# Operand tiles with 32 unused bytes behind each row tile

## The reference

```
u = rmsnorm(h) @ w_in            # 2048 x 5632
ya = silu(layernorm(conv31(a_val * sigmoid(a_glu)))) * silu(a_z)
yb = window_attention(q, k, v) * silu(b_z)
h = h + concat(ya, yb) @ w_out   # 2048 x 2048
h = h + rmsnorm(p @ w_pe) * sigmoid(h @ w_pg)
```

## Time and profile before

| | |
|---|---|
| median of 3 runs | 1776.14 us (1776.02, 1776.14, 1781.95) |
| span of the profiled execution | 1780.4 us |
| TensorE busy, weight loads | 1759.6, 1678.8 us |
| VectorE, ScalarE, GpSimd busy | 1312.3, 899.0, 39.9 us |
| DMA | 326.07 MB, 183 GB/s |

### The profile page before, as it was taken

How to read it: one execution, slowest core, us unless ns; L and a number is a source line. 1 busy time by engine, 2 the same in 40 slices (tenths; PEclk the granted TensorE clock), 3 DMA queues, 4 the chain that set the end, 5 groups by cost and what they waited for, 6 DMA issues and landing times.

```text
span 1780.4 us, 35691 instructions
## 1 busy us (share of the span) xinstructions
PE 1759.6 (99%) x14349; PEld 1678.8 (94%) x14349; DVE 1312.3 (74%) x2087; ACT 899.0 (50%) x1326; POOL 39.9 (2%) x48
## 2 busy tenths in 40 slices
PE   8999999999999999999999999999999999999997
PEld 8999999999999999999999899898989999999876
DVE  7899899976779987998677765556565657566754
ACT  5433665545544355556465454545455443655653
POOL 0000000000000000000000110000100000000000
PEclk9999999999999999999999999999999999999999
DMA  7666545555656665456556656665655566455553
GB/s 232 187 206 193 190 143 174 192 188 185 192 177 209 192 199 151 146 186 206 189 191 197 201 179 203 187 189 170 206 162 170 190 190 193 142 158 169 172 189 130
DMA packets 200082, 326.07 MB, mean 183 GB/s; under 512 B 14911, under 2 KB 66319, under 8 KB 199821
## 3 DMA queue, kind: packets, MB, share of 16 engines
q1 hardware_dynamic: 197085, 320.85, 58.0%
q10 hardware_dynamic: 2864, 3.36, 0.6%
HBM read 320.42 MB, written 2.69 MB: 181 GB/s over the span
## 4 chain that ended last, share of the span: by engine, by line
PE 86%; DVE 9%; ACT 1%; issue 1%; DMA 1%; ACTq 0%; DVEq 0%; SPq 0%
PE g L495 67%; PE g L506 11%; DVE w_lo L902 4%; DVE cacc L1148 3%; PE att L620 2%; PE att L641 2%; PE att L596 2%; DMA turned<-q 1%; ACT w_hi L1531 1%; ACTq L1519 0%; PE att L793 0%; DVE u L996 0%; DMA stage<-in_w_in_dram 0%; ACT L1540 0%; DVE q L923 0%
## 5 line engine op out<-in xcount | busy, mean ns | idle before, releaser
L902 DVE TENSOR_TENSOR w_lo<-stage,w_hi 128x1024 fp32r<-128x1024 f32 x577 | 707.6, 1234 | 388.8 <-ACT w_hi L1531 388.1
L1531 ACT CAST w_hi<-stage 128x1024 fp32r<-128x1024 f32 x577 | 598.2, 1050 | 595.3 <-PE g L495 373.7
L495 PE MATMUL g<-a_hi,w_hi 128*128 128x256 f32 x2496 | 703.9, 282 | 2.4 <-DVE w_lo L902 1.5
L495 PE MATMUL g<-a_hi,w_lo 128*128 128x256 f32 x2496 | 695.0, 278 | 0.0
L495 PE MATMUL g<-a_lo,w_hi 128*128 128x256 f32 x2496 | 694.9, 278 | 0.0
L495 PEld LDWEIGHTS g<-a_hi,w_hi 128*128 128x128 f32 x2496 | 472.1, 189 | 11.8 <-issue 9.5
L495 PEld LDWEIGHTS g<-a_lo,w_hi 128*128 128x128 f32 x2496 | 470.6, 189 | 0.0
L495 PEld LDWEIGHTS g<-a_hi,w_lo 128*128 128x128 f32 x2496 | 469.7, 188 | 0.5 <-issue 0.2
L495 PE MATMUL g<-b_hi,w_hi 128*128 128x256 f32 x1440 | 403.6, 280 | 0.4 <-DVE w_lo L902 0.3
L495 PE MATMUL g<-b_hi,w_lo 128*128 128x256 f32 x1440 | 400.4, 278 | 0.0
L495 PE MATMUL g<-b_lo,w_hi 128*128 128x256 f32 x1440 | 400.4, 278 | 0.0
(11 more groups left out here) (230 smaller groups left out, 1368.1 us busy)
## 6 DMA issues: line engine op xcount, KB each, us to landing
stage<-in_fox_w_in_dram SPq DMA_DIRECT2D x128, 512.0 KB, 3.8
stage<-in_w_in_dram SPq DMA_DIRECT2D x112, 512.0 KB, 3.8
stage<-in_swa_w_in_dram SPq DMA_DIRECT2D x72, 512.0 KB, 3.9
stage<-in_w_in_dram SPq DMA_DIRECT2D x128, 256.0 KB, 3.1
stage<-in_w_out_dram SPq DMA_DIRECT2D x64, 512.0 KB, 4.2
stage<-in_w_pg_dram SPq DMA_DIRECT2D x64, 512.0 KB, 3.9
stage<-in_fox_w_out_dram SPq DMA_DIRECT2D x32, 512.0 KB, 4.5
stage<-in_swa_w_out_dram SPq DMA_DIRECT2D x32, 512.0 KB, 4.0
```

Source lines behind the costliest of these rows:

```text
L495: mm = pe.matmul(acc[:, j * S:(j + 1) * S], w[:, slot, c0 + j * P:c0 + (j + 1) * P], xx[:, k, :], start=st and m == 0 and j % 2 == 0, stop ...
L902: dve.tensor_tensor(w_lo[:, slot, :], stage[:, slot, :], w_hi[:, slot, :].bitcast(F32), ALU.subtract).then_inc(*t.inc("w_split"))
L1531: act.copy(w_hi[:, slot, :], stage[:, slot, :]).then_inc(*t.inc("w_rounded"))
```

## The change

```diff
+SKEW = 8
 ...
         sb("apart", [APART])
-        a_hi = sb("a_hi", [KT, S], F32R)
-        a_lo = sb("a_lo", [KT, S], F32R)
-        b_hi = sb("b_hi", [KT, S], F32R)
-        b_lo = sb("b_lo", [KT, S], F32R)
+        a_hi = sb("a_hi", [KT, S + SKEW], F32R)[:, :, 0:S]
+        a_lo = sb("a_lo", [KT, S + SKEW], F32R)[:, :, 0:S]
+        b_hi = sb("b_hi", [KT, S + SKEW], F32R)[:, :, 0:S]
+        b_lo = sb("b_lo", [KT, S + SKEW], F32R)[:, :, 0:S]
```

## The result

The changed kernel takes 1811.68 us (four runs, 1810.75 to 1812.22), the kernel before 1777.23 us (four runs, 1776.02 to 1781.95): ratio 1.018, 95% interval 1.0161 to 1.0200. The profiled executions stand 30.0 us apart in their spans, less than the medians do, since the one of before was its longest.

A forecast was written before the change was run, and what follows sets the result against it. TensorE was taken to bound the kernel, mainly through 12,000 matmul pitches on line 495. +24 us of pitch, +22 after VectorE's hiding, with line 506 and writers 0, gave 1776.1 + 22 = 1798 us; range 1781 to 1820, wider 1758 to 1824.

The forecast's parts named there:

- mostly the long pitch with the short one found anew: The forecast's mechanism on line 495: short pitch found anew every 12 matmuls; +22 us, 1798 us, chance 0.54.
- The pitch of line 495: 12,000 matmuls on TensorE: mean pitch rises from 115.4 to 117.4 ns, +24 us before hiding.
- the chunk with changing places: Key and value chunk, six matmuls of line 495 and six of 506 in turn: 116.4 ns a step, +12 us.
- What of it is hidden: VectorE holds 9% of the chain, where slower matmuls cost nothing: 24 x 0.91 = +22 us.
- Line 506: Weights and operands change sides, 756 wide matmuls: between -7 and +7 us, taken as 0.
- The writers: ScalarE and VectorE writing four rows at a time, runs now broken: at worst +1.4 us, taken as 0.
- the 13 ns for a break: Cost of one break in a write, from glu's 694 against gate's 681 ns.
- The range: Likeliest case's own range: +5 to +44 us, 1781 to 1820 us; the wider range was 1758 to 1824.
- The long pitch loses its hold: Rival on line 495: most places free, streams soon fall into step; -23 to about -15 us, 1761 us, chance 0.25.
- Alignment has nothing to do with it: Rival: the two pitches come from phase alone, mix stays near half; 1776 us within 5, chance 0.12.
- A row that begins amid 64 bytes: Rival: operands read in 64-byte pieces, odd k need one more; +40 us on top, 1835 us, chance 0.09.
- The rule of the Trainium skill: Loading next weights takes no read bandwidth from the running matmul; by it the sum would be 0.

The follow-up runs named there:

- c_0: The kernel before with apart 64 bytes longer, so all 16 row tiles stand at 0 from the weights: 1827.54 us, ratio 1.0245.
- c_480: The kernel before with apart 32 bytes longer, so all row tiles stand at 480 from the weights: 1814.18 us, ratio 1.0171.
- s_64: The changed kernel with 64 unused bytes a row instead of 32: 1806.08 us, ratio 1.0148 to the kernel before.

## Why the prediction was right, and where its sizes were off

The direction was right, and so was where the cost lies: TensorE's pitch on line 495, by the place of row tile to weights. The signs named came true as well: means of 280 ns, no long stretch of one pitch, `w_lo` at 1235 ns against 1234. The mechanism, mostly the long pitch with the short one found anew, was right in part only, and the measured 1811.68 us lies 14 above the 1798. The step "The pitch of line 495" was too small. I took 117.4 ns, between the chunk with changing places and `pe`; it is 118.1. The premise under the 117.4 failed: that the short pitch can be found anew at many places after each change. In c_0 and c_480 nothing changes, and they are at 120.0 and 118.3 ns; in the changed kernel k = 2, at the place of c_0, ends at 120.0 (118.9 in the mean), and k = 1, at that of c_480, has 118.1. So most of the cost is that of the places, and settling doesn't help. A change has a part too: k = 0 and 8 stand where the kernel before stands and have 116.4 and 117.0 ns, against its 115.2. From 115.2 to 118.1 are 2.9 ns, times 12,000 = 35 us instead of 24. My 115.4 for the kernel before was 0.2 too high by the same sum.

*What of it is hidden* was too small as well: I took off 9%. The spans differ by 30.0 us, and 35 + 2.6 (next point) - 30.0 leaves some 7.5 us hidden, a fifth. VectorE's part of the chain fell by 4 points of the span: it waits more for ScalarE's casts, 411.6 against 388.1 us, and these wait more for TensorE.

*Line 506*, taken as 0 and at most +7: the wide form's mean pitch rises from 229.1 to 232.6 ns, 756 x 3.5 = +2.6 us. *The writers*, taken as 0: 0, their medians are 1048 and 1226 ns; the 13 ns for a break that I had from rows 12 doesn't carry over.

*The range* held, but its lower bound isn't what its words say: the chunk with changing places less what VectorE hides is 12 x 0.91 = +11, and +5 is reached only with the gain on line 506 that the words leave out.

Of the places: k = 14 has `pe`'s pitch (118.7 against 118.7 there) and k = 4 a long one (117.9), as said. That all 16 places differ was wrong, the period being 256 bytes: they are eight, twice each.

The rivals. *The long pitch loses its hold* was the closest to a true observation: it does, no stretch at 117.8 is left that spans tiles. But what comes instead is above the kernel before's 115.2 at all eight places, and above 117.8 itself at five of them (k = 1, 2, 3, 5, 6 and those 8 further). Nor did a pitch live for thousands of matmuls: the longest unbroken stretches of the kernel before are 1,066 steps long (383 to 508 us) and 1,015 short (851 to 966 us). *Alignment has nothing to do with it* is refuted by `pe` in c_0 and by c_480. *A row that begins amid 64 bytes* is refuted by c_0, c_480 and s_64. The rule of the Trainium skill that is weighed there ("TensorE: Matmul & The Clock Gate", Step-by-step: what each phase is for), that loading the next weights takes no read bandwidth from the running matmul, doesn't fit this stream: the same matmul beside the same loads lasts 276 or 281 ns at one and the same distance, and 283 ns with 64 bytes more (c_0's line below).

```profile
L495 PE MATMUL g<-a_lo,w_hi 128*128 128x256 f32 x2496 | 706.5, 283 | 0.0
```

What isn't shown is what collides inside. That the two reads of TensorE disturb each other is inferred from the dependence on their distance alone, and from the duration of one load in three, which grows too (192 against 188 ns). What puts a stretch on the one pitch or the other is open as well. A kernel with the loads taken away wasn't tried.

## What to carry to other kernels

Where matmuls with 4-byte operands run back to back, each with a weight load, look at the distance between starts in the timeline. Two values for one instruction were here the sign that operand and weights disturb each other, and the address of one against the other, modulo 256 bytes, was worth up to 2.5%. Here it was better to keep all tiles at the one best distance than to spread them over many: a spread averages over places, most of which were worse. And compare such kernels by several runs, since at one distance chunks fell into either pitch for up to 125 us on end.

## What the runs showed of the hardware that I had not expected

The pitch is a matter of state: with the distance unchanged it stays at 113.3 or 117.8 ns for up to a thousand matmuls, until something interrupts TensorE, and which of them follows differs between like chunks of one trace (117.4 and 113.0 ns in the two windows of the kernel before) and between kernels of one distance (973 or 937 matmuls in the same window). A matmul of 128 columns ahead of a chunk turned the pitch over in 26 of 28 cases; one of 32 columns mostly brought the long one. And the places are steps, not slopes: 432 and 448 are alike, 464 and 480 are alike, and between 448 and 464 lie 32 us of the whole kernel.
